# A quarter of a convolution's last span on GpSimd, and the softmax reciprocals of 15 of 20 attention steps spread through memory

## What is computed

```python
h = rms_norm(x, norm_mix) * (1 + scale1) + shift1        # shift, scale, gate: rows of silu(c) @ ada_w + ada_b
q, k, v, u = split(h @ w_in)                             # 8 query heads, 2 key/value heads, head size 64
q, k = apply_rope(rms_norm(q)), apply_rope(rms_norm(k))
p = softmax(q @ k.T * scale)                             # per head, 128 queries at a time
attn_out = p @ v
a = val * sigmoid(gate)                                  # val, gate: halves of u, 512 channels
y = conv(a, conv_w)                                      # depthwise, 31 taps, padding 15
conv_out = silu(layer_norm(y + conv_b))
x = x + gate1 * (concat([attn_out, conv_out]) @ w_out)
...                                                      # router, 16 experts, top-k, SwiGLU
```

## Time and profile before

| what | value |
|---|---|
| three timed runs | 1510.94, 1512.67, 1512.75 us; median 1512.67 us |
| the profiled execution, its own time | 1508.8 us |
| its span, first to last instruction | 1507.0 us (1.8 us lie around it) |
| PE, DVE, ACT, POOL busy | 1418.2, 1106.1, 798.6, 209.9 us |
| mean granted clock of PE | 0.976 |
| chain that ended last | PE 88%, DVE 5%, DMA 2% |
| transition, 288 to 349 us: PE, DVE, ACT busy | 48.8, 52.9, 21.9 of 61 us |
| attention, 349 to 563 us | 16 prompt steps of 12 us, 4 short sample steps |

### The profile page before, as it was taken

The page is one execution under the profiler, slowest core; times in us unless marked ns, Lnnn a source line. Parts: engine busy times, 40 slices in busy tenths (PEclk is TensorE's granted clock), DMA queues, the critical chain, the costliest instruction groups (busy, mean ns, idle before and its releaser), DMA issues.

```text
span 1507.0 us, 26861 instructions
## 1 busy us (share of the span) xinstructions
PE 1418.2 (94%) x9933; PEld 1066.8 (71%) x9933; DVE 1106.1 (73%) x1564; ACT 798.6 (53%) x1303; POOL 209.9 (14%) x211
## 2 busy tenths in 40 slices
PE   4999999978999998998499999999999999999996
PEld 1777787636887886876277777777777777777774
DVE  1258888988877887437678887778877787877884
ACT  2222222136777775223556766566665666756662
POOL 0022022100000000211102111221012210212110
PEclk8999999989999999999599999999999999999998
DMA  9400001273000001333888888989889898889951
GB/s 361 153 1 28 29 1 56 98 293 114 2 2 2 2 2 56 112 131 130 300 303 295 299 296 289 317 290 305 287 301 313 290 308 283 304 290 315 308 186 18
DMA packets 113682, 281.31 MB, mean 187 GB/s; under 512 B 10581, under 2 KB 16825, under 8 KB 110552
## 3 DMA queue, kind: packets, MB, share of 16 engines
q1 hardware_dynamic: 105944, 259.54, 48.2%
q0 software_dynamic: 7680, 20.98, 6.0%
HBM read 259.51 MB, written 20.97 MB: 186 GB/s over the span
## 4 chain that ended last, share of the span: by engine, by line
PE 88%; DVE 5%; DMA 2%; ACT 1%; POOL 1%; SPq 1%; issue 1%; DVEq 0%; ACTq 0%; POOLq 0%
PE banks L1455 12%; PE banks L1460 12%; PE banks L1456 12%; PE banks L1480 12%; PE banks L1135 9%; PE banks L1338 6%; PE banks L1146 6%; PE banks L1287 4%; PE banks L1262 4%; PE banks L1272 4%; DVE c_t L1677 2%; DMA ada<-in_ada_w 1%; PE banks L1510 1%; PE banks L1487 1%; PE banks L1299 1%; DMA xn_sample<-xn 1%
## 5 line engine op out<-in xcount | busy, mean ns | idle before, releaser
L2003 DVE TENSOR_TENSOR low<-raw,high 128x1024 fp32r<-128x1024 f32 x384 | 446.5, 1218 | 1.0
L985 ACT ACTIVATE high<-raw 128x1024 fp32r<-128x1024 f32 x384 | 380.4, 1051 | 9.6 <-issue 8.8
L1677 DVE SCALAR_TENSOR_TENSOR c_t<-a_t,taps,c_t 128x256 f32<-128x256 f32 (+2 forms) x360 | 215.0, 660 | 0.5
L1455 PE MATMUL banks<-high,x_hi 128*128 128x512 f32 x512 | 207.9, 406 | 0.0
L1456 PE MATMUL banks<-high,x_lo 128*128 128x512 f32 x512 | 200.5, 392 | 0.0
L1460 PE MATMUL banks<-low,x_hi 128*128 128x512 f32 x512 | 158.3, 390 | 1.1 <-DVE low L2003 1.1
L1135 PE MATMUL banks<-h_t,w_u 128*128 128x256 f32 x640 | 143.9, 382 | 2.9 <-ACT h_t L735 2.9
L1135 PEld LDWEIGHTS banks<-h_t,w_u 128*128 128x128 f32 x640 | 121.1, 192 | 18.9 <-issue 3.1
L1480 PE MATMUL banks<-raw,xs_t 128*32 128x256 f32 x2048 | 118.3, 383 | 0.0
L1455 PEld LDWEIGHTS banks<-high,x_hi 128*128 128x128 f32 x512 | 96.1, 188 | 31.1 <-issue 13.6
L1775 DVE TENSOR_REDUCE negmax<-banks 128x1 f32<-128x1024 f32 (+1 forms) x80 | 84.9, 1062 | 41.4 <-PE banks L1262 41.2
(11 more groups left out here) (230 smaller groups left out, 2128.2 us busy)
## 6 DMA issues: line engine op xcount, KB each, us to landing
raw<-in_w_gate SPq DMA_DIRECT2D x128, 512.0 KB, 4.2
raw<-in_w_up SPq DMA_DIRECT2D x128, 512.0 KB, 5.3
raw<-in_w_down SPq DMA_DIRECT2D x64, 1024.0 KB, 5.0
ada<-in_ada_w SPq DMA_DIRECT2D x24, 1024.0 KB, 8.6
w_u<-in_w_in SPq DMA_DIRECT2D x4, 1024.0 KB, 18.3
x_in<-in_x_prompt SPq DMA_DIRECT2D x4, 1024.0 KB, 4.9
w_out_sb<-in_w_out SPq DMA_DIRECT2D x1, 4096.0 KB, 13.0
x_again<-in_x_prompt SPq DMA_DIRECT2D x4, 1024.0 KB, 5.9
```

The costliest lines, as they stand in the source:

```text
L985: act.activation(high[c % RING][:, :], raw[ph][:, k, :], ACT.Copy).then_inc(hi_ready, 1)
L1455: pe.matmul(bank(b + h), s_hi_k, w_high[:, half], start=(k == 0), stop=False)
L1677: dve.scalar_tensor_tensor(out=c_t[s][:, c, :], in0=a_t[:, c, bass.ds(k + o, n)], scalar=taps[:, c, bass.ds(k, 1)], in1=c_t[s][:, c, :], o ...
L2003: dve.tensor_tensor(low[ph][:, k, :], raw[ph][:, k, :], high[c % RING][:, :].bitcast(F32), ALU.subtract).then_inc(lo_ready, 1)
```

## The change

1. **Convolution.** Span 2's last column (`c` = 3) moves to POOL, after its last rotation: one multiply-and-add with the bias, and for each further tap a multiplication into `tap_of` and an addition, 61 instructions over 640 tokens, each waiting for the one before. From the second on they wait for the last `mod_step`, whose buffer `tap_of` lies in. DVE keeps three columns; `AHEAD` is 4, so 12 instructions stand in the transition and 81 in attention, five a step.
2. **Reciprocals.** In 15 steps (prompt steps that a prompt step of the same key/value head follows, and the last sample step) PE and ACT have no part in them. SP stores the 128 x 4 reciprocals to memory, one element at a time (`h q -> q h`), waits for it, and loads them back twice, each load repeating rows over 64 partitions. `inv_rows` has two buffers.
3. **Transition.** PE's order is another: `mod_step` 2 to 7 of the second set now stand ahead of the second span's `mean` and of the last tile's `turn_q`; two of the third set stand ahead of `variance(1)`. Two of DVE's splits stand ahead of the last rotation's sum, and its `centre`s ahead of all taps of span 2. ACT's `copy_rows(1)` is earlier. The third set's turning (`mod_turn(2, 7)`) moves into step 0, behind the first turned probabilities, and the DVE instructions that read it behind the third maximum.
4. Four small semaphores are dropped or merged.

```diff
+        def through_memory(s):
+            return s < STEPS - 1 and steps[s][2] == 0 and steps[s + 1][2] == 0 or s == phases[3][3] - 1
+        TAP_COLS = (CC, CC, CC - 1)
...
+            for s in range(STEPS):
+                if through_memory(s):
+                    m = in_memory(s)
+                    by_head = inv_d[s].rearrange("(c i) q -> i c q", i=2)
+                    sp.wait_ge(sums_inverted, s + 1)
+                    sp.dma_start(inv_d[s].rearrange("h q -> q h"), inv[:, s % 2, :], allow_slow_non_contiguous=True).then_inc(inv_stored, 16)
+                    sp.wait_ge(inv_stored, 16 * (m + 1))
+                    if s >= 2:
+                        sp.wait_ge(mixed, s - 1)
+                    for i in range(2):
+                        sp.dma_start(inv_rows[s % 2][HD * i:HD * (i + 1), :, :], by_head[i].partition_broadcast(HD)).then_inc(inv_loaded, 16)
...
+            pool.tensor_scalar(c_t[2][:, c, :], a_t[:, c, o:o + n], taps[:, c, 0:1], cols[:, ROW_CB + c:ROW_CB + c + 1],
+                               ALU.mult, ALU.add).then_inc(conv_last, 1)
+            pool.wait_ge(rows_ready, 3)
+            for k in range(1, TAPS):
+                pool.wait_ge(conv_last, 2 * k - 1)
+                pool.tensor_scalar(tap_of[:, :], a_t[:, c, o + k:o + k + n], taps[:, c, k:k + 1], None, ALU.mult).then_inc(conv_last, 1)
+                pool.wait_ge(conv_last, 2 * k)
+                pool.tensor_tensor(c_t[2][:, c, :], c_t[2][:, c, :], tap_of[:, :], ALU.add).then_inc(conv_last, 1)
...
-                    if s and h == 1:
+                    if s and h == 1 and not through_memory(s - 1):
                         inv_t_out(s - 1)
-                    if s and h == 3:
+                    if s and h == 3 and not through_memory(s - 1):
                         inv_rows_out(s - 1)
...
             mod_step(1, 1, ada2[1], 2)
-            turn_last_q()
-            mean(1)
-            for k in range(2, 4):
+            turn_q(NPAIR - 1, 0, 0)
+            turn_q(NPAIR - 1, 0, 1)
+            for k in range(2, 6):
                 mod_step(1, k, ada2[k], 2)
-            variance(0)
...
+            pe.wait_ge(qkv_copied, 2 * NT)
+            mean(1)
+            turn_q(NPAIR - 1, 1, 0)
+            turn_q(NPAIR - 1, 1, 1)
+            variance(0)
             mod_turn(1, 7)
+            turn_q(NPAIR - 1, 1, 2)
+            for k in range(2):
+                mod_step(2, k, ada2[k], 3)
+            variance(1)
...
-                    if s and h == 2:
+                    if s and h == 2 and not through_memory(s - 1):
                         spread_inv(s - 1)
                     if s and h == 0:
                         weigh(s - 1, 1)
-                        turn_inv(s - 1)
+                        if not through_memory(s - 1):
+                            turn_inv(s - 1)
...
-            AHEAD = 7
-            centre(0)
-            some_taps(2, 0, 2 * CC)
-            centre(1)
+            AHEAD = 4
+            some_taps(2, 0, 2 * TAP_COLS[2])
             scale_span(0)
-            some_taps(2, 2 * CC, 5 * CC)
+            some_taps(2, 2 * TAP_COLS[2], AHEAD * TAP_COLS[2])
             dve.wait_ge(rows_turned, 2)
             mod_cols(1)
             scale_span(1)
-            some_taps(2, 5 * CC, AHEAD * CC)
...
             def mix(s):
...
-                dve.wait_ge(inv_rows_copied, s + 1)
+                if through_memory(s):
+                    dve.wait_ge(inv_loaded, 32 * (in_memory(s) + 1))
+                else:
+                    dve.wait_ge(inv_rows_copied, on_tensor(s) + 1)
```

More of the change, by code:

```diff
@@ L168, in encoder_layer @@
     mix_t = put("mix_t", [P, CC, TOK], F32, Z1 + 57344)
[L169 to L172, removed]
+    inv_rows = [put(f"inv_rows{i}", [P, 2, P], F32, o) for i, o in enumerate((Z1 + 77824, at["small"] + 8192))]
+    sums = put("sums", [P, 2, QPK], F32, Z1 + 78848)
+    inv = put("inv", [P, 2, QPK], F32, Z1 + 78880)
+    inv_t = put("inv_t", [QPK, P], F32, at["small"] + 8192 + D)
+    tap_of = put("tap_of", [P, SPANS[2][1]], F32, Z1 + 79360)
     sq_c = [put(f"sq_c{i}", [P, CC, SPANS[i][1]], F32, o) for i, o in enumerate((Z1 + 16384, Z1 + 20480, Z1 + 45056))]
@@ L454, in encoder_layer, with on_tensor, in_memory, inv_taken @@
         assert len(steps) == STEPS
+        def through_memory(s):
+            return s < STEPS - 1 and steps[s][2] == 0 and steps[s + 1][2] == 0 or s == phases[3][3] - 1
+        def on_tensor(s):
+            return sum(not through_memory(i) for i in range(s))
+        def in_memory(s):
+            return sum(through_memory(i) for i in range(s))
+        def inv_taken(dve, s):
+            if through_memory(s):
+                dve.wait_ge(inv_stored, 16 * (in_memory(s) + 1))
+            else:
+                dve.wait_ge(inv_turned, on_tensor(s) + 1)
+        TAP_COLS = (CC, CC, CC - 1)
         def mixed_by(q):
@@ L829, in gate_row_out @@
                 act.activation(gate1_row[:, n // 2, 512 * (n % 2):512 * (n % 2) + 512], bank(4 + n % 2), ACT.Copy).then_inc(gate_rows_copied, 1)
+            for i in range(3):
+                high_out(NPAIR - 1, 0, i)
             squares(0)
+            copy_rows(1)
+            for i in range(3):
+                high_out(NPAIR - 1, 1, i)
             squares(1)
@@ L1194, in _ @@
             pe.wait_ge(u_gated, CC * NPAIR)
[L1195 to L1199, removed]
             def mean(s):
                 for c in range(CC):
-                    pe.wait_ge(conv_done[s], CC * (TAPS - 1) + c + 1)
+                    if c < TAP_COLS[s]:
+                        pe.wait_ge(conv_done[s], TAP_COLS[s] * (TAPS - 1) + c + 1)
+                    else:
+                        pe.wait_ge(conv_last, 2 * TAPS - 1)
                     for b, c0, c1 in STAT_BANK[s]:
@@ L1304, in _ @@
             scores(0)
-            pe.wait_ge(mod_ready, 2)
-            mod_turn(2, 7)
+            pe.wait_ge(rows_copied, 3)
             scores(1)
@@ L1313, in _ @@
                     turn_probs(n + h, h, nt)
-                    if s and h == 2:
+                    if s == 0 and h == 0:
+                        pe.wait_ge(mod_ready, 2)
+                        mod_turn(2, 7)
+                    if s and h == 2 and not through_memory(s - 1):
                         spread_inv(s - 1)
@@ L1682, in some_taps @@
                 for i in range(first, last):
-                    tap(s, i % CC, i // CC)
+                    tap(s, i % TAP_COLS[s], i // TAP_COLS[s])
             BESIDE = 40
@@ L1733, in _ @@
                 beside(p, 35, BESIDE)
-                qk_norm(2 * p + 1)
-            for a in range(2):
-                for i in range(3):
-                    low_out(NPAIR - 1, a, i)
+                qk_norm(2 * p + 1, (0, 1) if p == NPAIR - 1 else ())
             def centre(s):
@@ L1754, in scale_span @@
                     dve.tensor_tensor(c_t[s][:, c, :], c_t[s][:, c, :], rs_c[s][:, :], ALU.mult).then_inc(scaled, 1)
+            low_out(NPAIR - 1, 0, 2)
+            centre(0)
+            low_out(NPAIR - 1, 1, 0)
+            low_out(NPAIR - 1, 1, 1)
+            centre(1)
+            low_out(NPAIR - 1, 1, 2)
             dve.wait_ge(u_gated, CC * NPAIR)
@@ L1822, in step_taps @@
                         first, last = (LATE * (3 * (PROMPT_TILES * j + l) + i) // (3 * PROMPT_STEPS) for i in (m, m + 1))
-                        some_taps(2, CC * AHEAD + first, CC * AHEAD + last)
+                        some_taps(2, TAP_COLS[2] * AHEAD + first, TAP_COLS[2] * AHEAD + last)
                 maximum_of(n + 2)
+                if s == 0:
+                    dve.wait_ge(rows_turned, 3)
+                    mod_cols(2)
+                    dve.wait_ge(mod_ready, 3)
+                    scale_of(a2, ROW_NFFN, SCALE2)
                 if s >= 2:
```

78 lines of the change are left out of this document (40 added, 38 removed).

## The result

The changed kernel takes 1518.38 us (median of 20 runs, 1511.13 to 1524.05), the kernel before 1512.62 us beside it (20 runs, 1508.71 to 1514.7): a ratio of 1.0043, 95% interval 1.0029 to 1.0056. It is slower, by 5.8 us. The forecast of 1496 us, its range and its sign were all wrong. The profiled execution of the changed kernel, 1511.13 us with a span of 1509.3, is the fastest of its 20 runs, so what follows shows the loss at its smallest. The runs scatter over 13 us, those of before over 6.

The account below looks back on a forecast made before the run. It took PE's instructions to bound attention's prompt steps and the chain through DVE to bound the transition. Transition 8.9 plus reciprocals 8.7 less POOL 1.0 made 16.6 us, from 1512.67 to 1496 us, range 1488 to 1512.

Parts of the forecast that it names:

- its sign: Whole kernel: faster than before, given a chance of 0.80; within the measurement's resolution 0.07, slower 0.13.
- I take 2.3 for the store and 2.3 for both loads: Attention, reciprocals' trip through memory: about 5 us with the two issues, taken as hidden, so costing nothing.
- The upper end: Attention: the trip's upper end, three times about 5 us, taken as just about hidden by some 15 us of cover.
- Rival 4: Attention: trip through memory late from 15 us on; at 17 us it costs 30 us, giving 1526; chance 0.03.
- The cover: Attention: `mix(s)` comes some 15 us behind `invert(s)` in DVE's order, time in which the trip is hidden.
- Transition: Transition: scores behind the first exponent at 341.5 instead of 350.90, 9.4 us less; 8.9 after 0.5 for step 0.
- PE's 15 x 0.58: Attention: PE loses four spreading matmuls, 0.58 us, in each of 15 prompt steps, gaining 8.7 us.
- POOL: POOL's convolution quarter delays DVE: +1.0 us over eight attention steps, and half of 1.25 at the transition's scaling.
- the first rival: Attention: POOL gets in between a group's taps, 4.4 us of waits a step, giving about 1513 or half, 1504; chance 0.17.
- the 2.2 us free in a step: Attention: DVE's free time a step, 2.0 + 0.8 less the 0.6 by which the step shortens, covering waits for POOL.
- the forecast's rule: Attention: three groups of taps a step each wait half a POOL instruction of 1.25 us, 1.8 us; groups mostly stay whole.
- The sum: Whole kernel: 8.9 + 8.7 - 1.0 = 16.6 us less, giving 1496 us; forecast's chance 0.47.

Follow-up runs that it names:

- e7: Kernel before, with only the 15 steps' reciprocals spread from SBUF to SBUF; convolution all on DVE, old transition: 1503.3 us, 0.9944 of before.
- e6: e4 with POOL's 30 later convolution taps left out, so the output isn't the reference's: 1492.02 us, 0.9870 of before.
- e5: Changed kernel, its store written as 128 pieces of 16 bytes instead of 512 of 4; output isn't the reference's: 1494.98 us, 0.9889 of before.
- e10: Changed kernel, each 4-byte piece stored in 64 bytes of its own; loads read a copy filled with ones: 1496.3 us, 0.9883 of before.
- e3: Changed kernel, but PE turns and ACT copies the reciprocals and SP stores four rows of 512 bytes: 1495.38 us, 0.9896 of before.
- e4: e3 without memory: four DMAs a step repeat the turned rows over 64 partitions from SBUF to SBUF: 1494.38 us, 0.9894 of before.
- e2: Kernel before, with only the reciprocals' trip through memory added; convolution and transition as they were: 1524.57 us, 1.0088 of before.

## Why the prediction was wrong

**The step that failed** is "I take 2.3 for the store and 2.3 for both loads, about 5 us with the two issues", with "So the trip is hidden at either end of its range". The 2.3 was read from the earlier trace rows, a load of 64-byte pieces into SBUF; nothing in the trace of before was a store of 4-byte pieces to memory, and a load said nothing of it. Measured, the store waits 9.4 us, the first trip takes 14.3 and the second 20.3. Two faults sit in it. The upper end, three times 5, was put just where the cover ends and then treated as safe: a bound that touches the cover needed a chance of its own, not 0.03. And the loads were costed as if nothing else were under way: with late stores the second load took 10.0 to 12.6 us in three steps, where I had 2.3 for both, and only the two together make the trips of 20 us. SP's one queue also pushed stores back, by up to 2.7 us behind their reciprocals, but by no more than 0.8 in the three long trips.

Rival 4, "The trip through memory is late", is what happened: DVE's `mix` waits for DMA, with the maxima queued behind it, from 14 to 15 us on. Its price, 2 us in each of 15 steps, came near in size (30 forecast, 19 in the profiled execution, 23 in the medians), but that is luck, for the form is another: most trips are covered or up to 4 us over, and the three with a late load are 6.7 to 7.9 over.

**The cover** of some 15 us was put too high: the first trip, 14.3 us, delayed `mix` by 0.4, so 13.9 were covered; in the second it was 13.4, and in the last step of the first prompt half 10.8 (a trip of 14.6, a wait of 3.8). The upper end of my range stood over the cover, not at it.

**Transition**: forecast 9.4 us at the scores (8.9 with step 0's share), measured 9.7. Of these 0.65 were there ahead of the transition: its first sums start at 297.69, before at 298.34, and over all runs this start lies between 297.5 and 300.5 us. So 9.0 are the transition's own. The scaling was done at 337.5 (forecast 337.8), with ACT's copy, table and exponent behind it as written down. That it fits so well is in part luck: `centre(1)` ended 1.0 us and PE's last block, at 331.6, some 2 us ahead of their forecast, while POOL held the scaling up by 1.9 us where I had 0.6. (A tap of 0.81 is 0.80 by its row, 0.1 us in all.)

**PE's 15 x 0.58**: forecast 8.7, measured 8.5 (e7, interval 6.4 to 10.6).

**POOL**: forecast +1.0 in attention and 0.6 in the transition; e6 gives 1.2 and 1.6 us. Mis-sized was the instruction: the multiplication, put at 1.25 us as its upper end, takes 1.88 at the least and 2.13 in the mean, the addition 1.53 and 1.60 (two views of one line each, ns min/median/max, of the changed kernel):

```profile
L681 POOL TENSOR_SCALAR tap_of<-a_t,taps x30: 1883/2332/2456, 331.7 to 445.5; 128x640 f32<-128x640 f32 x30
```

```profile
L683 POOL TENSOR_TENSOR c_t<-c_t,tap_of x30: 1529/1552/1917, 333.7 to 447.5; 128x640 f32<-128x640 f32 x30
```

On the waits the rows lie between my forecast and the first rival: 2.5 us a step (20.2 over eight), against 1.8 forecast and 4.4 by that rival; the 2.2 us free in a step were nearly enough. Three groups of taps a step, each waiting for half of a POOL instruction of 1.6 or 2.1 us, make 2.8: with the right size, the forecast's rule gives about what was measured. The Trainium skill, SBUF — State Buffer, "Who interferes with whom", says that the shared port pair is an exclusive lock and that the order of issue decides who blocks. Read strictly, POOL's waiting instruction would go in ahead of every next tap; 0.5 us more a tap, for POOL instructions of 1.6 and 2.1, says that a group mostly waits only for one under way.

**The sum**: e5 and e10, which have all parts of the change but the late store, stand at 0.9889 and 0.9883 of before, 16.8 and 17.7 us less, where the sum was 16.6 (e3 and e4, which also give the right values, 15.7 and 16.0 less). The other terms were right within 1.2 us each, in part by errors that cancel, and the one put at nothing decided.

## What to carry to other kernels

A transfer that replaces work on an engine is costed by a row of the same kind: same direction, same size of piece, same neighbours in memory; where there is none, measure it by itself, as one store awaited by an otherwise idle queue does. The DMA's busy share says nothing of a late landing. A round trip is costed with what else is on the queue at that time, here the next step's store, and its cover is counted at the step where it is shortest. Before handing single elements of 128 partitions to memory, group them to 16 bytes, give each 64 bytes of its own, or turn them first; of the three only turning them first (e3, e4) was run with loads that bring the right values.

## What the runs showed of the hardware

- A store's landing depends on what its pieces have for neighbours: 512 pieces of 4 bytes from 128 partitions landed in 8.7 to 11.3 us side by side (in e2 one was waited for 12.1) and in 2.3 to 3.4 us when 64 bytes apart; even 128 such pieces side by side took 7.6 to 7.8. The packets are moved alike: 528 of them are over 1.3 us after the store's issue in the changed kernel and 1.7 after it in e10, and from there to the landing it is 7.5 us side by side and 0.9 apart. The Trainium skill, DMA: Bandwidth & Descriptors, "Specifications", says that transfers under 512 bytes are done as read-modify-write. No run here shows that mechanism itself; it would fit neighbours that are served one after the other, but by the page's limit the pieces that lie apart, and the 16-byte ones, would be late as well, and they aren't.
- Late loads go with late stores. With the 4-byte pieces side by side the slowest load took 12.6 us (the changed kernel) and 12.3 (e2); with prompt stores 3.8 (e3), 3.9 (e5, which reads what a 16-byte store had just written) and 3.3 (e10). In the changed kernel the next step's store had gone out within 0.8 us behind each of the three late loads, but five other loads with a store as close took 2.7 to 4.8. By what way the store delays the load is not shown.
- After 3.15 us without work PE came back with a granted clock of 0.69 over 5.5 us, against 1.00 ahead of it and behind it.
